# Two mix norms turned by transposes, the attention loop's transposes and masks in another order

## The chip, the cores and the metric

The kernel runs on 1 core of a Trainium2 chip. The time is the device time of one execution in microseconds (us). Engines: TensorE (PE in the rows, its weight loads PEld), VectorE (DVE), ScalarE (ACT), GpSimd (POOL), SyncE (SP), which issues the weight loads from HBM.

## The reference

Three transformer layers over 512 tokens of width 1024, in fp32. The change touches two places of the first two layers. After the mixer of layer 0 (a convolution block) and of layer 1 (attention) comes

```
x = layer_norm(DN_ALPHA * x + mix, ln_mix_g[i], ln_mix_b[i])     # (x - mean) * rsqrt(var + eps) * g + b
ffn = conv_gated_ffn(x, ...)
ple = sigmoid(x @ ple_w_gate[i]) * (p[i] @ ple_w_proj[i])
x = layer_norm(DN_ALPHA * x + ffn + ple, ...)
```

and layer 1 mixes with stick-breaking attention, 16 heads of 64:

```
z = einsum(q, k) * scale;  mask = key < query
log_1m = where(mask, log_sigmoid(-z), 0)
log_a = log_sigmoid(z) + (cumulated log_1m of the later keys)
a = where(mask, exp(log_a), 0);  out = a @ v;  mix = out @ b_wo
```

## The kernel before

**Products.** Each fp32 weight chunk (128x1024) is split into a high and a low part: SP loads `raw`, ScalarE makes `wH` (`high`, L1053), GpSimd `wL` (L416), and TensorE forms three products (L458 to L460, or `by_tokens`, L484 to L486). Four slots hold the chunks, and a chunk's high part is made three chunks ahead: `high_after(c)` waits for the end of chunk c and makes chunk c + 3. Semaphores order everything by hand; each engine runs its list in program order.

**Mix norm** (`mix_norm` on ScalarE, `ple` on TensorE, and a part of VectorE's list; once for layer 0, `mix0`, once for layer 1, `mix1`). The residual stream lies in four blocks of 128 tokens x 1024 (`xr`). For each block VectorE adds the product (L1588), forms the negative mean and writes `xg` = (x - mean) * g (`centre_block`, L1597; the rows call it tmp, whose memory it shares). ScalarE squares the block with its sum (`deviation`, L1129), takes the inverse deviation with Ln and Exp (L1113, L1117), and scales a 128x128 identity by it into `turner` (L1124). TensorE then turns the block to channels x tokens: `turn_block` (L495) does 8 fp32 products of a 128x128 piece of `xg` with `turner`, which divides and turns at once. Blocks 0 and 1 are turned first, then 2 and 3 into the same banks. Out of the banks ScalarE writes the high part `xH` with the shift b added (`high_tiles`, L1170) and VectorE the low part `xL` (`low_tiles`, L1626). Meanwhile TensorE projects p for the four blocks (`project_p`, banks 0 to 3 by turns), and ScalarE keeps each of them in `proj` (`keep`, L1196). Then comes the gate product (`gate`), which needs `xH`, `xL`, all four kept projections and the weight chunks. Off that path VectorE writes the normed stream itself, `xr` = xg * deviation + b (`finish_block`, L1604).

**Attention** (`pair`, once for each of 8 pairs of heads p). On TensorE: `scores` in three parts (`PARTS3`: query tile 3; tiles 2 and 0; tile 1), each part with its masks (a bf16 product into the bank, L723) and its scores (L730), two heads each. Then, for the next pair, the projections of q and k (`project`, 24 products each), `turn_weights(p, 0)` (8 transposes, L742), the projection of v, `turn_weights` 1 and 2 (12 transposes), `turn_values` (4 transposes of v into bank 7, L712), and at last `values`, the weighted sum (L752, L756), which needs all turned weights. On ScalarE: the sigmoids (`chances`, L1325, L1328), copies of q, k, v, of turned weights (`copy_weights`, L1335) and turned v (`copy_values`, L1316), and of the result (`mH`, L1352). On VectorE: the scans (L1755) and the weights (`weigh`, L1762). The last pair has no next pair and fills its waits with small products (`keep_warm`).

Of the kernel before, what the change touches and what calls it, by code (L numbers as in the profile page):

```python
# [8 lines left out]
ACT = mybir.ActivationFunctionType  # L9
ALU = mybir.AluOpType  # L10
# [116 lines left out]
def build_block(nc, ws, xT, xN, pT, params, consts, rope, w1, rows, out):  # L127
    with ExitStack() as ctx:
# [325 lines left out]
        def _(pe):  # L454
# [32 lines left out]

            def turn_block(xname, q, src):

                h = q // 2  # L490
                pe.wait_ge(x_normed, QT * TURN[xname] + q + 1)
                for n in range(KT):
                    bank = ps[TURN_BANKS[xname][h][n // 2]]
                    o = (n % 2) * 2 * P + (q % 2) * P
                    mm = pe.matmul(bank[:, o:o + P], src(q)[:, n * P:n * P + P], turner[:, q, :], start=True, stop=True)  # L495
                    if q % 2 and n % 2:
                        mm.then_inc(x_turned, 1)

            def centred(name):
                def src(q):  # L500
                    pe.wait_ge(x_centred, QT * LN_OF[name] + q + 1)
                    return xg[:, q, :]
                return src

            def updated(q):
                return xr[:, q, :]

            def first_chunks(outs, c, name, xname, src, turn_at, fill):

# [111 lines left out]
            def ple(layer, xname):  # L621

                c0 = CHUNK[f"ple{layer}"]
                full = FULL[("pw2", "wo")[layer]]
                pe.wait_ge(p_ready, layer + 1)
                pe.wait_ge(low_ready, c0 + 2)
                for q in range(2):
                    pe.wait_ge(block_taken, 8 * full + 2 * q + 2)
                    project_p(layer, q).then_inc(proj_done, 1)
                pe.wait_ge(block_taken, 8 * full + 8)  # L630
                src = centred(("pw2", "wo")[layer])
                turn_block(xname, 0, src)
                turn_block(xname, 1, src)
                for q in range(2, QT):
                    pe.wait_ge(proj_kept, QT * layer + q - 1)
                    mm = project_p(layer, q)
                    if q < QT - 1:
                        mm.then_inc(proj_done, 1)
                pe.wait_ge(x_ready, XV[xname] + KT)
                turn_block(xname, 2, src)  # L640
                turn_block(xname, 3, src)

                def gate(k, qs, last=False):
                    c = c0 + 2 + k
                    pe.wait_ge(low_ready, c + 1)
                    for q in qs:
                        t = slice(q * P, q * P + P)
                        for half in range(2):
                            mm = by_tokens(ps[2 * q + half], c % SLOTS, half, xH[:, k, t], xL[:, k, t], k == 0, last)
                            if last and (q, half) != (QT - 1, 1):  # L650
                                mm.then_inc(gate_done, 1)
                    return mm

                pe.wait_ge(proj_kept, QT * layer + QT)
                for k in range(2):
                    pe.wait_ge(x_ready, XV[xname] + k + 1)
                    gate(k, (0, 1))
                pe.wait_ge(x_ready, XV[xname] + 2 * KT)
                for k in range(2):
                    pe.wait_ge(x_ready, XV[xname] + KT + k + 1)  # L660
                    gate(k, (2, 3)).then_inc(chunk_done, 1)
                for k in range(2, KT):
                    pe.wait_ge(x_ready, XV[xname] + KT + k + 1)
                    gate(k, range(QT), k == KT - 1).then_inc(chunk_done, 1)
# [50 lines left out]
            def scores(p, j):  # L715


                for n, tiles in enumerate(PARTS3):
                    if p:
                        pe.wait_ge(bT_ready, 3 * (p - 1) + n + 1)  # L720
                    for h in range(2):
                        for i, (qt, o, w) in enumerate(tiles):
                            pe.matmul(ps[2 * n + h][:, o + w - P:o + w], maskSB, identB, start=i == 0, stop=False,  # L723
                                      skip_group_check=True)
                    if n == 0:
                        pe.wait_ge(qkv_copied, p * 4 + 2)
                    for i, (qt, o, w) in enumerate(tiles):
                        for h in range(2):
                            r = slice(DH * h, DH * h + DH)
                            mm = pe.matmul(ps[2 * n + h][:, o:o + w], qT[r, j, qt * P:qt * P + P], kT[r, j, 0:w],  # L730
                                           start=False, stop=False, skip_group_check=True)
                            if i == len(tiles) - 1:
                                mm.then_inc(z_ready, 1)
# [25 lines left out]
            def pair(p, j, more, first=False):  # L759
                scores(p, j)  # L760
                if more:
                    project(p + 1, 1 - j, 0)
                    project(p + 1, 1 - j, 1)
                    turn_weights(p, 0)
                    project(p + 1, 1 - j, 2)
                    turn_weights(p, 1)
                    turn_weights(p, 2)
                    turn_values(p + 1, 1 - j)
                else:
                    pe.wait_ge(qkv_copied, p * 4 + 4)  # L770
                    keep_warm(7, 30)
                    turn_weights(p, 0)
                    keep_warm(7, 15)
                    turn_weights(p, 1)
                    keep_warm(7, 8)
                    turn_weights(p, 2)
                    keep_warm(7, 6)
                if not first:
                    pe.wait_ge(m_ready, p)
                pe.wait_ge(qkv_copied, p * 4 + 4)  # L780
                values(p, j)

            first_chunks((ps[7], ps[6]), c0, "down0", "ffn0", centred("down0"), (4, 6), 3)
            project(0, 0, 2)
# [261 lines left out]
        def _(act):  # L1046
# [88 lines left out]
            def unit_block(name, q):  # L1135
                deviation(name, q)
                turning_matrix(name, q, 4)

            def post_block(name, q):

                if q < QT - 1:
                    act.wait_ge(block_done, (QT - 1) * FULL[name] + q + 1)
                else:
                    act.wait_ge(chunk_done, CHUNK[name] + dict(COUNTS)[name])
                act.activation(squares[:], banks[:, 2 * q:2 * q + 2, :].rearrange("p a b -> p (a b)"), ACT.Square,  # L1145
                               accum_out=figure(name, q, 3)).then_inc(post_sum, 1)
                act.wait_ge(post_sum, QT * FULL[name] + q + 1)
                inverse_std(name, q, 3, 4, 1)
                act.sem_inc(post_std, 1)
# [36 lines left out]
            def mix_norm(layer):  # L1186
# [13 lines left out]
                    act.wait_ge(res_step, QT)  # L1200
                load_row(f"mix_b{layer}", b_row[:])
                high(c0 + 1)
                for q in range(QT):
                    unit_block(name, q)
                high_after(c0 - 1)
                keep(0)
                high_tiles(xname, 0, 0, 2, shift=f"mix_b{layer}")
                keep(1)
                high(c0 + LEAD)
                high_tiles(xname, 0, 2, 4, shift=f"mix_b{layer}")  # L1210
                keep(2)
                keep(3)
                high_tiles(xname, 1, 0, 4, shift=f"mix_b{layer}")

            def ple(layer):
# [122 lines left out]
            def pair(p, j, more):  # L1338
                for n in range(3):
                    chances(p, n)  # L1340
                if more:
                    copy_qkv(p + 1, 1 - j, 0)
                    copy_qkv(p + 1, 1 - j, 1)
                copy_weights(p, 0)
                if more:
                    copy_qkv(p + 1, 1 - j, 2)
                copy_weights(p, 1)
                copy_weights(p, 2)
                if more:
                    copy_values(p + 1, 1 - j)  # L1350
                act.wait_ge(av_ready, p * 2 + 2)
                act.activation(mH[:, bass.ds(p, 1), :].rearrange("p o t -> p (o t)"), ps[6][:], ACT.Copy)\  # L1352
                    .then_inc(m_high, 1)

            act.sem_inc(q_free, 1)
            for which in range(3):
# [193 lines left out]
        def _(dve):  # L1550
# [43 lines left out]
            def centre_block(name, q):  # L1594
# [2 lines left out]
                dve.scalar_tensor_tensor(xg[:, q, :], xr[:, q, :], figure(name, q, 2), g_row, ALU.add, ALU.mult)\  # L1597
                    .then_inc(x_centred, 1)

            def finish_block(name, q):  # L1600

                dve.wait_ge(post_std, QT * FULL[name] + q + 1)
# [128 lines left out]
                low_tiles("mix0", h, 0, 4, shift="mix_b0")  # L1731
            dve.wait_ge(row_loaded["mix_b0"], 16)
            for q in range(QT):
                finish_block("pw2", q)
            ple(0)
            ffn(0)
            dve.wait_ge(row_loaded["ffn_g0"], 16)
# [50 lines left out]
                low_tiles("mix1", h, 0, 4, shift="mix_b1")  # L1788
            dve.wait_ge(row_loaded["mix_b1"], 16)
            for q in range(QT):  # L1790
                finish_block("wo", q)
            ple(1)
            ffn(1)

# [372 lines left out]
```

## Time and profile before

| | |
|---|---|
| time, median of 3 runs | 2419.19 us (2417.32 to 2421.7) |
| profiled execution | 2417.3 us, its span 2415.5 us |
| busy: PE, DVE, ACT, POOL | 2356.6 (98%), 912.2 (38%), 950.2 (39%), 955.9 (40%) us |
| mean granted clock of TensorE | 0.997 |

Busy time is read from the span between the first and the last instruction; a clock of 1.00 is 2.4 GHz. In a timeline the first number is the start in us from the span's start, the second the length in us of the piece, xN the records merged into it (an fp32 product of TensorE is two records, a transpose one), and in brackets the engine's idle time before it and what ended it.

### The profile page before, as it was taken

The page shows a single profiled execution, that of the slowest core. Times are in us where ns is not written, and L with a number is a line of the kernel's source. Part 1 is how long each engine was busy: PE and PEld are TensorE (multiplying, and loading weights), DVE is VectorE, ACT ScalarE, POOL GpSimd, SP SyncE. Part 2 cuts the span into 40 slices and gives each one's busy share as a digit, 9 for nine tenths or more (in the row PEclk, how much of TensorE's full clock was granted, in tenths as well). Part 3 has the DMA queues.
Part 4 walks back from the last instruction along what each step waited for, and adds up shares of the span by engine and source line. Part 5 has one row for each costly group of instructions (what it writes and reads, how often), then busy time and mean ns, then how long its engine had stood idle before and what let it go on. Part 6 is the DMA issues. An engine that isn't in the chain of part 4 may idle for free.

```text
span 2415.5 us, 30601 instructions
## 1 busy us (share of the span) xinstructions
PE 2356.6 (98%) x11320; PEld 1912.9 (79%) x11320; DVE 912.2 (38%) x1167; ACT 950.2 (39%) x1612; POOL 955.9 (40%) x422
## 2 busy tenths in 40 slices
PE   8989999999999999999999999999999989999998
PEld 6858888888877778888888888888877658888887
DVE  6985344420343323544400422210556862232201
ACT  7764333322454434433322522221534564322222
POOL 5834444444422223444444344444322103444443
PEclk9999999999999999999999999999999999999999
DMA  5212322222212122322222223223312002322222
GB/s 184 70 40 95 119 96 96 96 96 96 88 53 68 64 79 88 113 97 98 99 92 92 89 99 98 96 92 100 146 64 69 28 1 79 105 96 96 96 96 96
DMA packets 58755, 215.17 MB, mean 89 GB/s; under 512 B 6448, under 2 KB 6448, under 8 KB 58416
## 3 DMA queue, kind: packets, MB, share of 16 engines
q1 hardware_dynamic: 55440, 199.83, 24.7%
q10 hardware_dynamic: 3232, 14.16, 1.6%
q8 instruction: 62, 1.02, 0.2%
q14 instruction: 21, 0.17, 0.0%
HBM read 211.86 MB, written 2.10 MB: 89 GB/s over the span
## 4 chain that ended last, share of the span: by engine, by line
PE 87%; DVE 7%; ACT 3%; issue 2%; DMA 1%; SPq 0%; POOL 0%; DVEq 0%; ACTq 0%; POOLq 0%
PE banks L458 17%; PE banks L459 17%; PE banks L460 17%; PE banks L484 9%; PE banks L486 9%; PE banks L485 9%; DVE banks L1708 3%; PE banks L495 1%; PE banks L857 1%; PE banks L730 1%; PE banks L752 1%; PE banks L900 1%; ACT tmp L1473 1%; DMA raw<-ws 1%; PE banks L812 0%
## 5 line engine op out<-in xcount | busy, mean ns | idle before, releaser
L416 POOL TENSOR_TENSOR wL<-raw,wH 128x1024 fp32r<-128x1024 f32 x369 | 892.8, 2421 | 1423.3 <-ACT wH L1053 1423.1
L1053 ACT ACTIVATE wH<-raw 128x1024 fp32r<-128x1024 f32 x371 | 393.2, 1060 | 1108.8 <-PE banks L460 607.1
L458 PE MATMUL banks<-xH,wH 128*128 128x512 f32 (+1 forms) x1976 | 762.7, 386 | 13.3 <-DVE xL L1552 10.8
L459 PE MATMUL banks<-xL,wH 128*128 128x512 f32 (+1 forms) x1976 | 756.2, 383 | 0.0
L460 PE MATMUL banks<-xH,wL 128*128 128x512 f32 (+1 forms) x1976 | 756.1, 383 | 0.0
L458 PEld LDWEIGHTS banks<-xH,wH 128*128 128x128 f32 x1976 | 371.7, 188 | 93.7 <-DVE wL L1557 10.8
L460 PEld LDWEIGHTS banks<-xH,wL 128*128 128x128 f32 x1976 | 371.8, 188 | 72.8
L459 PEld LDWEIGHTS banks<-xL,wH 128*128 128x128 f32 x1976 | 371.9, 188 | 71.5 <-issue 0.7
L484 PE MATMUL banks<-wH,hH 128*128 128x512 f32 x704 | 274.2, 389 | 3.5 <-DVE tmp L1666 3.5
L486 PE MATMUL banks<-wL,hH 128*128 128x512 f32 x704 | 273.9, 389 | 0.0
L485 PE MATMUL banks<-wH,hL 128*128 128x512 f32 x704 | 273.9, 389 | 0.0
L1668 DVE TENSOR_TENSOR hL<-tmp,hH 128x512 f32 x88 | 206.0, 2341 | 98.3 <-ACT hH L1257 98.3
L1666 DVE TENSOR_TENSOR tmp<-banks,tmp 128x512 f32<-128x512 f32 x88 | 60.9, 692 | 365.2 <-PE banks L460 354.0
L484 PEld LDWEIGHTS banks<-wH,hH 128*128 128x128 f32 x704 | 132.1, 188 | 32.4 <-issue 5.1
L485 PEld LDWEIGHTS banks<-wH,hL 128*128 128x128 f32 x704 | 132.2, 188 | 27.4
L486 PEld LDWEIGHTS banks<-wL,hH 128*128 128x128 f32 x704 | 132.2, 188 | 27.3
L1659 DVE SCALAR_TENSOR_TENSOR tmp<-banks,par,tmp 128x511 f32<-128x511 f32 x88 | 65.9, 749 | 139.2 <-ACT tmp L1247 132.5
L1588 DVE SCALAR_TENSOR_TENSOR xr<-xr,banks 128x512 f32<-128x512 f32 x32 | 20.6, 680 | 259.1 <-PE banks L486 259.1
L1612 DVE TENSOR_TENSOR banks<-banks,tmp 128x512 f32<-128x512 f32 x24 | 15.5, 692 | 259.5 <-ACT squares L1145 259.2
L1708 DVE SCALAR_TENSOR_TENSOR banks<-gpad,par,banks 128x512 f32<-128x512 f32 x112 | 75.1, 750 | 1.1 <-DVE tmp L1682 0.9
L484 PE MATMUL banks<-wH,xH 128*128 128x512 f32 x192 | 75.0, 390 | 0.0
L486 PE MATMUL banks<-wL,xH 128*128 128x512 f32 x192 | 74.7, 389 | 0.0
(247 smaller groups left out, 2275.1 us busy)
## 6 DMA issues: line engine op xcount, KB each, us to landing
raw<-ws SPq DMA_DIRECT2D x371, 512.0 KB, 3.6
w1b<-w ACTq DMA_DIRECT2D x2, 2048.0 KB, 11.4
tmp<-rows ACTq DMA_DIRECT2D x7, 512.0 KB, 3.3
b_row<-rows ACTq DMA_DIRECT2D x5, 512.0 KB, 4.4
tmp<-xT SPq DMA_DIRECT2D x8, 256.0 KB, 7.4
xr<-xN ACTq DMA_DIRECT2D x1, 2048.0 KB, 8.6
out<-xr SPq DMA_DIRECT2D x4, 512.0 KB, 2.6
pf<-pT ACTq DMA_DIRECT2D x2, 512.0 KB, 3.8
```

The source lines that it names most:

```text
L416: pool.tensor_tensor(wL[:, j, :], raw[:, j, :], fp(wH[:, j, :]), ALU.subtract).then_inc(low_ready, 1)
L458: pe.matmul(bank, wH[:, slot, cols], rh, start=start, stop=False)
L459: pe.matmul(bank, wH[:, slot, cols], rl, start=False, stop=False)
L460: return pe.matmul(bank, wL[:, slot, cols], rh, start=False, stop=stop)
L484: pe.matmul(bank, rh, wH[:, slot, w], start=start, stop=False)
L485: pe.matmul(bank, rl, wH[:, slot, w], start=False, stop=False)
L486: return pe.matmul(bank, rh, wL[:, slot, w], start=False, stop=stop)
L1053: act.activation(wH[:, c % SLOTS, :], raw[:, c % SLOTS, :], ACT.Copy).then_inc(high_ready, 1)
L1659: dve.scalar_tensor_tensor(tmp[:, j, back:S], ps[4 + 2 * j][:, 0:S - back], pc(f"fcw{inst}", f * FCONV_W + tap), tmp[:, j, back:S], ALU.mu ...
L1666: dve.tensor_tensor(tmp[:, 2 + j, :], ps[5 + 2 * j][:], tmp[:, j, :], ALU.mult).then_inc(h_made, 1)
L1668: dve.tensor_tensor(hL[:, bass.ds(f, 1), :].rearrange("p o t -> p (o t)"), tmp[:, 2 + j, :], fp(hH[:, bass.ds(f, 1), :].rearrange("p o t - ...
L1708: ins = dve.scalar_tensor_tensor(dst, g, w, sums[i % 2], ALU.mult, ALU.add)
```

## The change

In the mix norms ScalarE multiplies the centred block by the deviation (`divide_block`), TensorE turns it with a plain transpose against the identity, and VectorE adds b to it for the stream (`shift_block`). ScalarE's list in `mix_norm` is ordered anew. In the attention the three `turn_weights` follow each other ahead of the third projection, `turn_values` and its copy come behind `values` and the copy of the result, and the masks of all three parts stand together ahead of the scores.

```diff
@@ turn_block
+                    if src is divided:
+                        mm = pe.transpose(bank[:, o:o + P], xg[:, q, n * P:n * P + P], cc("ident"))
+                    else:
+                        mm = pe.matmul(bank[:, o:o + P], src(q)[:, n * P:n * P + P], turner[:, q, :], start=True, stop=True)
...
@@ ple, TensorE
-                src = centred(("pw2", "wo")[layer])
-                turn_block(xname, 0, src)
-                turn_block(xname, 1, src)
+                turn_block(xname, 0, divided)
+                turn_block(xname, 1, divided)
...
-                turn_block(xname, 2, src)
-                turn_block(xname, 3, src)
+                turn_block(xname, 2, divided)
+                turn_block(xname, 3, divided)
@@ scores
+                if p:
+                    pe.wait_ge(bT_ready, 3 * p)
                 for n, tiles in enumerate(PARTS3):
-                    if p:
-                        pe.wait_ge(bT_ready, 3 * (p - 1) + n + 1)
                     for h in range(2):
                         for i, (qt, o, w) in enumerate(tiles):
                             pe.matmul(ps[2 * n + h][:, o + w - P:o + w], maskSB, identB, start=i == 0, stop=False,
                                       skip_group_check=True)
-                    if n == 0:
-                        pe.wait_ge(qkv_copied, p * 4 + 2)
+                pe.wait_ge(qkv_copied, p * 4 + 2)
+                for n, tiles in enumerate(PARTS3):
                     for i, (qt, o, w) in enumerate(tiles):
@@ pair, TensorE
-                    turn_weights(p, 0)
+                    for n in range(3):
+                        turn_weights(p, n)
                     project(p + 1, 1 - j, 2)
-                    turn_weights(p, 1)
-                    turn_weights(p, 2)
-                    turn_values(p + 1, 1 - j)
...
                 values(p, j)
+                if more:
+                    turn_values(p + 1, 1 - j)
@@ ScalarE
+            def divide_block(name, q):
+
+                deviation(name, q)
+                act.wait_ge(x_centred, QT * LN_OF[name] + q + 1)
+                act.activation(xg[:, q, :], xg[:, q, :], ACT.Copy, scale=figure(name, q, 4)).then_inc(x_normed, 1)
@@ mix_norm
-                for q in range(QT):
-                    unit_block(name, q)
+                for q in range(3):
+                    divide_block(name, q)
+                keep(0)
+                divide_block(name, 3)
+                keep(1)
                 high_after(c0 - 1)
-                keep(0)
-                high_tiles(xname, 0, 0, 2, shift=f"mix_b{layer}")
-                keep(1)
-                high(c0 + LEAD)
-                high_tiles(xname, 0, 2, 4, shift=f"mix_b{layer}")
+                high_tiles(xname, 0, 0, 4, shift=f"mix_b{layer}")
                 keep(2)
                 keep(3)
+                high(c0 + LEAD)
                 high_tiles(xname, 1, 0, 4, shift=f"mix_b{layer}")
@@ pair, ScalarE
-                copy_weights(p, 0)
+                for n in range(3):
+                    copy_weights(p, n)
                 if more:
                     copy_qkv(p + 1, 1 - j, 2)
-                copy_weights(p, 1)
-                copy_weights(p, 2)
-                if more:
-                    copy_values(p + 1, 1 - j)
                 act.wait_ge(av_ready, p * 2 + 2)
                 act.activation(mH[:, bass.ds(p, 1), :].rearrange("p o t -> p (o t)"), ps[6][:], ACT.Copy)\
                     .then_inc(m_high, 1)
+                if more:
+                    copy_values(p + 1, 1 - j)
@@ VectorE
+            def shift_block(xname, q):
+
+                dve.wait_ge(x_normed, QT * TURN[xname] + q + 1)
+                dve.tensor_tensor(xr[:, q, :], xg[:, q, :], b_row[:], ALU.add).then_inc(res_step, 1)
...
-                finish_block("pw2", q)
+                shift_block("mix0", q)
...
-                finish_block("wo", q)
+                shift_block("mix1", q)
```

## Rows read from the trace of the kernel before

**Rows 1.** The page, chain that ended last, by engine.
```profile
PE 87%; DVE 7%; ACT 3%; issue 2%; DMA 1%; SPq 0%; POOL 0%; DVEq 0%; ACTq 0%; POOLq 0%
```
**Rows 2.** Timeline of TensorE in one pair of the attention; start, length.
```profile
712.38 2.16 PE L752 MATMUL banks<-bT,vN 128*64 128x384 f32 x16 [1.38 <-ACT bT L1335]
...
714.69 0.28 PE L723 MATMUL banks<-bcon 128*128 128x128 bf16 x2
714.90 1.13 PE L730 MATMUL banks<-kT,qT 64*128 64x512 f32 x4
715.96 0.40 PE L723 MATMUL banks<-bcon 128*128 128x128 bf16 x4
716.29 1.14 PE L730 MATMUL banks<-kT,qT 64*128 64x384 f32 x8
717.36 0.28 PE L723 MATMUL banks<-bcon 128*128 128x128 bf16 x2
...
718.21 0.50 PE L458 MATMUL banks<-xH,wH 128*128 128x512 f32 x1
...
729.24 1.04 PE L742 MATMUL banks<-con,beta 128*128 128x128 f32 x8
...
735.70 1.47 PE L742 MATMUL banks<-con,beta 128*128 128x128 f32 x12
737.00 0.60 PE L712 MATMUL banks<-con,vT 128*128 128x128 f32 x4
738.98 0.54 PE L752 MATMUL banks<-bT,vN 128*64 128x384 f32 x2 [1.38 <-ACT bT L1335]
```
**Rows 3.** Waits of TensorE from 650 to 905 us: in total, times, longest.
```profile
PE banks L752 <- ACT bT L1335: 9.7, 7, 1.4
```
**Rows 4.** Timeline of VectorE and ScalarE in the same pair.
```profile
725.80 0.73 DVE L1762 TENSOR_TENSOR beta<-banks,beta 128x255 f32<-128x255 f32 x2
...
738.72 0.61 ACT L1316 ACTIVATE vN<-banks 128x512 f32<-128x512 f32 x1
```
**Rows 5.** Timeline of TensorE in the first mix norm.
```profile
218.74 3.73 PE L495 MATMUL banks<-turner,tmp 128*128 128x128 f32 x32
...
227.76 3.73 PE L495 MATMUL banks<-turner,tmp 128*128 128x128 f32 x32
...
231.25 0.48 PE L484 MATMUL banks<-wH,xH 128*128 128x512 f32 x1
```
**Rows 6.** Timelines of ScalarE, VectorE and GpSimd in the first mix norm.
```profile
208.30 1.13 ACT L1129 ACTIVATE squares<-xr,stat 128x1024 f32<-128x1024 f32 x1
209.34 0.18 ACT L1129 ACTIVATION_READ_ACCUMULATOR squares<-xr,stat 128x1 f32 x1
...
210.22 0.41 ACT L1124 ACTIVATE turner<-con,stat 128x128 f32<-128x128 f32 x1
210.53 1.14 ACT L1129 ACTIVATE squares<-xr,stat 128x1024 f32<-128x1024 f32 x1
...
219.43 1.00 ACT L1196 ACTIVATE proj<-banks 128x1024 f32<-128x1024 f32 x1
...
230.19 3.03 ACT L1170 ACTIVATE xH<-banks,par 128x256 fp32r<-128x256 f32 x8 [1.21 <-PE banks L495]
...
231.07 3.23 DVE L1626 SCALAR_TENSOR_TENSOR xL<-banks,par,xH 128x256 fp32r<-128x256 f32 x8 [4.04 <-ACT xH L1170]
...
224.68 2.40 POOL L416 TENSOR_TENSOR wL<-raw,wH 128x1024 fp32r<-128x1024 f32 x1 [2.72 <-ACT wH L1053]
```
**Rows 7.** Timelines of ScalarE and TensorE in the second mix norm.
```profile
904.14 1.13 ACT L1129 ACTIVATE squares<-xr,stat 128x1024 f32<-128x1024 f32 x1
...
923.55 3.73 PE L495 MATMUL banks<-turner,tmp 128*128 128x128 f32 x32
```
**Rows 8.** Groups by form: busy us, mean ns of one, idle before and its cause.
```profile
L1643 DVE TENSOR_TENSOR tmp<-tmp,proj 128x1024 f32<-128x1024 f32 x8 | 18.6, 2320 | 63.9 <-issue 63.9
```
**Rows 9.** Windows: length, then busy us (records) of each engine, clock, DMA share, GB/s.
```profile
735.00:739.00 4.00, 2.62 (x22) 2.23 (x20) 0.00 (x0) 3.11 (x5) 1.49 (x1) 1.00 0.38 131
```

More of the change, by code:

```diff
@@ L494, in turn_block @@
                     o = (n % 2) * 2 * P + (q % 2) * P
-                    mm = pe.matmul(bank[:, o:o + P], src(q)[:, n * P:n * P + P], turner[:, q, :], start=True, stop=True)
+                    if src is divided:
+                        mm = pe.transpose(bank[:, o:o + P], xg[:, q, n * P:n * P + P], cc("ident"))
+                    else:
+                        mm = pe.matmul(bank[:, o:o + P], src(q)[:, n * P:n * P + P], turner[:, q, :], start=True, stop=True)
                     if q % 2 and n % 2:
@@ L506, in updated, with divided @@
                 return xr[:, q, :]
+            def divided(q):
+                return xg[:, q, :]
             def first_chunks(outs, c, name, xname, src, turn_at, fill):
```

## The prediction, made before the change was run

> **What bounds the kernel now.** I read the page first, then the waits of TensorE, then the two stretches that the change touches as a timeline. The chain that ended last is TensorE's for 87% of the span [rows 1], so an edit is worth what it takes out of TensorE's own order of work: instructions there, or waits there. Work of ScalarE, VectorE and GpSimd counts only where TensorE waits for it.
>
> In the attention loop one pair takes 738.98 - 712.38 = 26.6 us, seven pairs of eight alike. TensorE's row shows four bits of mask and score work, then 729.24 - 718.21 = 11.0 us of two projections, 8 turned weight tiles, the third projection, 12 turned tiles, 4 turned values, and then a hole before the weighted values start at 738.98 [rows 2]. The hole is the only wait of that loop that TensorE has on another engine: 1.4 us, seven times, for the copy of the turned weights, 9.7 us in all [rows 3]. The copy can't come sooner, because its transposes are the last thing before the values.
>
> At the mix norm TensorE never waits. It turns two token blocks from 218.74, projects for two blocks, turns the other two from 227.76, and starts the gate at 231.25 [rows 5]. Those turnings are ordinary fp32 products against a scaled identity: 16 of them (32 records, two passes each) in 231.25 - 227.76 = 3.49 us, 0.218 us each.
>
> **Part 1, values behind the third projection.** The transposes of parts 1 and 2 move ahead of the projection, so their copies on ScalarE lie under it: three, of at most 1.00 us each by the copy of 128x1024 from PSUM in [rows 6], against half of the 11.0 us of two projections, 5.5. The values then start with no wait. The turned v moves behind the values. From the start of the v transposes to the start of the values is now 738.98 - 737.00 = 1.98 us; of this the four transposes themselves are 4 x 0.108 = 0.43 us (12 transposes take 737.00 - 735.70 = 1.30 us) [rows 2]. What is left is 1.55; I take 1.5, since the transition to the next kind of product must be paid once. 7 pairs x 1.5 = **10.5 us**. Bounds: the wait alone, 9.7, and 7 x 1.55 = 10.9.
>
> What is late next? The transposes of parts 1 and 2 now need VectorE's weights earlier, straight after part 0's. VectorE ends its last weights at 725.80 + 0.73 = 726.53, TensorE arrives at 729.24 [rows 2, 4]: 2.7 us in hand. The masks put together push the first finished scores back by about 0.35 us and bring TensorE's arrival forward by 0.6, so 1.7 us remain, and parts 0 and 1 have more. Behind the values, ScalarE copies mH and then the turned v, two copies of 128x512 at 0.61 us each (the v copy's row in [rows 4]), before the next pair's sigmoids. It is through some 1.3 us after the values end. Until the first scores of the next pair TensorE needs 0.43 us of transposes, 0.57 of masks (below) and half or all of 1.06 of scores, 1.5 to 2.1 us, so the sigmoids wait for scores and not for the copies. The projection that reuses bank 7 comes over 3 us after the values. The high parts of weights behind each projection keep their places and run three chunks ahead; SP's loads follow the same counter.
>
> **Part 2, masks together.** Starts in [rows 2]: a group of two masks takes 714.90 - 714.69 = 0.21 us, one of four 716.29 - 715.96 = 0.33. So a mask costs 0.06 and a group 0.09. The scores: two heads of 512 columns 1.06, two of 384 and two of 128 (as many columns, twice the instructions) 1.07, two of 256 columns 718.21 - 717.36 - 0.21 = 0.64 [rows 2]. The second and the first differ by nothing, the third gives 0.42 us for 256 columns, and so 0.22 us belong to the group, not to its columns or instructions. Three groups of each become one: 2 x (0.09 + 0.22) = 0.62 us less a pair. Eight pairs, the last too: **4.9 us**. Below, if the cost of a group is a fill of the array that the scores of each part pay anyhow: 0; no row shows grouped masks. I take the upper value, because the scores of part 1 already show two tiles behind each other without a second such cost.
>
> **Part 3, the mix norms (twice).** A turning by transpose costs what one of the attention costs, 0.108 us; 16 of them 1.73 against 3.49 us. Four such stretches would give 4 x 1.76 = 7.0 us if TensorE could use it all. The records of the second site carry the same length, 3.73 us for 32 [rows 5, 7].
>
> ScalarE pays. It now multiplies a 128x1024 block by the deviation where it scaled a 128x128 identity. Before, the scaling costs 210.53 - 210.22 = 0.31 us of its order, the nearest row of the new shape is the square of the same block: its next instruction starts 209.34 - 208.30 = 1.04 later [rows 6]. So a block, now 210.53 - 208.30 = 2.23 us, takes 2.96. From 208.30: three blocks to 217.18, first projection kept (about 1.0, the row at 219.43) to 218.15, block 3's square and figures 1.92 to 220.07, its scaling to 221.11, second projection kept to 222.1, the weights' high part to 223.05, and eight tiles in 3.03 to 226.1. VectorE's last low tile ends 1.08 us behind ScalarE's last (234.30 against 233.22) [rows 6], so 227.16. TensorE: first turning ends at 218.74 + 1.73 = 220.5, two projections take 5.53 (227.76 less 218.74 + 3.49), the second turning could start at 226.0 but gets its banks at 227.2 to 227.4. A wait of about 1.3 us is new. The gate starts at 229.15 in place of 231.25: 2.1 us. In the second norm the first square lies 923.55 - 904.14 = 19.4 us before the second turning [rows 7], here 227.76 - 208.30 = 19.5, so the same gain. **4.2 us** together. Bounds: 7.0 with no wait, 2.5 if each step of ScalarE is 0.1 us longer than taken.
>
> Two edits cost nothing. The chunk whose high part is made behind the third and fourth kept projections, later than now, is ready on ScalarE at about 229.1 and on GpSimd 2.4 us later (row at 224.68) at 231.6 [rows 6]; the gate asks for it at 229.15 + 2.76 = 231.9. That is 0.3 us, the thinnest cover of the change: without it each us of lateness is a us of the time, twice. VectorE's last pass, a sum of two SBUF tiles in place of a multiply and add, may take 2.3 us as the product of the same shape does, but VectorE stands idle 32 us behind it [rows 8]; four of them fit.
>
> **The sum** is 10.5 + 4.9 + 4.2 = 19.6 us. The profiled execution took 2417.3 us, its span 2415.5 and 1.8 around it; so 2397.7. The median of the runs is 2419.19, 1.9 above it: forecast **2399.6 us**.
>
> **A rule that speaks against it.** In [rows 9] the stretch with 16 transposes and the hole behind them, over 3 us without one ordinary product, has a granted clock of 1.00, the level of 2.4 GHz, and what follows runs at the same pace. The Trainium skill (TensorE: Matmul & The Clock Gate, Part 4: PE-mode transpose) says that a transpose doesn't count as work of TensorE for the clock in the way a matmul does. By that rule 20 in a row, or 16 where products stood, could drop it; by the row they don't, since the longest such stretch of the new order (20 transposes, 2.2 us) is shorter than the one shown.
>
> **Rivals.** A, masks together give nothing: 19.6 - 4.9, so 2404.5. For it: the price of a group is read from three differences; against: two pairs of them agree.
> B, the norms give nothing, because ScalarE and the thin cover on GpSimd eat the shorter turnings: 2403.8. For it, the 0.3 us; against, that ScalarE would have to come 2 us later than its rows add up to.
> C, the wait moves to the transposes of parts 1 and 2, because VectorE's weights come late: if all of the hole comes back, 2417.3 - 9.1, so about 2410 in the median. It needs VectorE 1.7 + 1.5 us later than its rows.
> D, slower: the clock falls to 1.2 GHz in the runs of transposes. Twice 64 x 0.108 (norms) and twice 7 x 20 x 0.108 (weights) add 22 us, more than the 19.6 won, and each ordinary product behind them that runs slow comes on top; 2.5 us of these and the kernel is slower than 2424. Against it is the row of part 1's hole.
>
> **How the numbers follow.** Forecast 0.64, A 0.14, B 0.09, C 0.04, D 0.04, and 0.05 for what I haven't seen, split over small gain and none. About 0.2%, 4.8 us, is what a measurement of this kernel can tell from no change. The forecast, A, B and C are all beyond it on the fast side: 0.91; within 0.05; slower 0.04. The range: at its fast end all upper bounds, 10.9 + 4.9 + 7.0 = 22.8, give 2419.2 - 22.8 = 2396.4; at its slow end A with the lower norms, 10.5 + 0 + 2.5, gives 2406.2. About 1.5 us for the spread of the runs goes on both ends. 2395 to 2408.
>
> **What would show it.** Right: no idle of TensorE before the weighted values in seven pairs; a pair in 26.6 - 2.1 = 24.5 us; eight masks in 0.57 us and the scores in 2.3; turnings of 16 records in about 1.8 us; an idle of about 1.3 us before the second turning, put down to VectorE's low tiles. Wrong: TensorE waiting for beta before a transpose, waiting for GpSimd in the gate, scores as long as now, or a clock below 1.00 in a window of the loop. The prediction fails if a wait that I place on ScalarE's side lands on TensorE in every pair.

## The result, and the profile after

The changed kernel takes 2398.69 us (median of 4 runs, 2397.98 to 2399.91), the kernel before 2418.26 in the same series (4 runs, 2416.87 to 2421.7). The ratio is 0.9918, 95% interval 0.9900 to 0.9935: 19.6 us less. The profiled execution took 2399.91 us, its span 2398.1.

The page, the chain that ended last (beside [rows 1]):

```profile
PE 92%; ACT 4%; DVE 3%; DMA 1%; issue 1%; SPq 0%; DVEq 0%; ACTq 0%
```

**One pair of the attention.** The timeline of TensorE, as in [rows 2]:

```profile
708.91 0.66 PE L718 MATMUL banks<-con,vT 128*128 128x128 f32 x4
709.41 0.61 PE L729 MATMUL banks<-bcon 128*128 128x128 bf16 x8
709.95 2.43 PE L736 MATMUL banks<-kT,qT 64*128 64x512 f32 x16
712.30 0.50 PE L458 MATMUL banks<-xH,wH 128*128 128x512 f32 x1
...
723.33 2.35 PE L748 MATMUL banks<-con,beta 128*128 128x128 f32 x20
725.43 0.48 PE L458 MATMUL banks<-xH,wH 128*128 128x512 f32 x1
...
731.08 2.16 PE L758 MATMUL banks<-bT,vN 128*64 128x384 f32 x16
733.39 0.66 PE L718 MATMUL banks<-con,vT 128*128 128x128 f32 x4
```

From one turning of v to the next it is 733.39 - 708.91 = 24.48 us, where it was 26.6. No bracket stands behind the values: the hole is gone. Eight masks begin at 709.41 and the scores at 709.95, so 0.54 us for the masks; the scores take 712.30 - 709.95 = 2.35. Together 2.89 where six pieces took 3.52 [rows 2]. The list of waits from 650 to 905 us, where [rows 3] had seven of 1.4 us, now holds one wait in all, at the first turning of v, which the kernel before has too:

```profile
PE banks L718 <- ACT vT L1321: 0.7, 1, 0.7
```

VectorE and ScalarE in the same pair (beside [rows 4]):

```profile
720.85 0.73 DVE L1778 TENSOR_TENSOR beta<-banks,beta 128x255 f32<-128x255 f32 x2
...
709.06 0.60 ACT L1361 ACTIVATE mH<-banks 128x512 fp32r<-128x512 f32 x1 [0.81 <-PE banks L762]
709.61 0.60 ACT L1328 ACTIVATE vN<-banks 128x512 f32<-128x512 f32 x1
711.11 1.09 ACT L1337 ACTIVATE beta<-banks 128x512 f32<-128x512 f32 x2 [0.90 <-PE banks L736]
```

VectorE ends its weights at 721.58 and TensorE asks for them at 723.33: 1.75 us in hand. The sigmoids wait 0.90 us for TensorE's scores, not for the two copies ahead of them.

**The mix norms.** TensorE in the first and in the second (as [rows 5] and [rows 7]):

```profile
219.83 1.91 PE L497 MATMUL banks<-con,tmp 128*128 128x128 f32 x16
221.50 0.48 PE L484 MATMUL banks<-wH,pH 128*128 128x512 f32 x1
...
228.58 1.97 PE L497 MATMUL banks<-con,tmp 128*128 128x128 f32 x16 [1.39 <-DVE xL L1642]
230.30 0.48 PE L484 MATMUL banks<-wH,xH 128*128 128x512 f32 x1
...
897.96 1.91 PE L497 MATMUL banks<-con,tmp 128*128 128x128 f32 x16
906.29 1.97 PE L497 MATMUL banks<-con,tmp 128*128 128x128 f32 x16 [0.94 <-DVE xL L1642]
908.01 0.48 PE L484 MATMUL banks<-wH,xH 128*128 128x512 f32 x1
```

A turning takes 221.50 - 219.83 = 1.67 us where it took 3.49. From the first turning to the gate it is 230.30 - 219.83 = 10.47 us, before 231.25 - 218.74 = 12.51 [rows 5]: 2.04 less. In the second norm it is 908.01 - 897.96 = 10.05 us, before 12.52: 2.47 less. The bracket at 228.58 is a new wait, for VectorE's low tiles.

ScalarE, VectorE and GpSimd there (as [rows 6]):

```profile
209.53 1.14 ACT L1135 ACTIVATE squares<-xr,stat 128x1024 f32<-128x1024 f32 x1
...
211.44 1.15 ACT L1149 ACTIVATE tmp<-tmp,stat 128x1024 f32<-128x1024 f32 x1
212.50 1.13 ACT L1135 ACTIVATE squares<-xr,stat 128x1024 f32<-128x1024 f32 x1
...
234.13 4.62 DVE L1614 TENSOR_TENSOR xr<-tmp,b_row 128x1024 f32<-128x1024 f32 x4
...
230.30 2.41 POOL L416 TENSOR_TENSOR wL<-raw,wH 128x1024 fp32r<-128x1024 f32 x1 [3.28 <-ACT wH L1059]
234.17 6.83 POOL L416 TENSOR_TENSOR wL<-raw,wH 128x1024 fp32r<-128x1024 f32 x1 [1.46 <-ACT wH L1059]
```

The multiplication costs ScalarE 212.50 - 211.44 = 1.06 us of its order, a block 212.50 - 209.53 = 2.97. GpSimd's split of the gate's second chunk ends at 232.71, 0.3 us before the gate asks for it (230.30 + 2.76 = 233.06). The next split, of the gate's third chunk, takes 6.83 us instead of 2.4: it began 0.04 us behind the first of four sums of VectorE (4.62 us in one piece), and 4.58 + 2.25 is its length. In the kernel before, VectorE's four multiply-adds stand in the place of the sums, from 234.21, and the same split, begun just as close behind the first of them, takes 3.49 us:

```profile
234.25 3.49 POOL L416 TENSOR_TENSOR wL<-raw,wH 128x1024 fp32r<-128x1024 f32 x1 [7.17 <-ACT wH L1053]
```

That I had not expected, and the experiments return to it.

**A yardstick without the clock.** From the first turning of the first mix norm to the first turning at the end of layer 1, both kernels run at a granted clock of 1.00, so this distance D tells more than one whole execution. Its end in the kernel before, then in the changed one:

```profile
1331.96 2.02 PE L495 MATMUL banks<-turner,xr 128*128 128x128 f32 x16 [0.57 <-ACT turner L1124]
```
```profile
1312.95 2.02 PE L499 MATMUL banks<-turner,xr 128*128 128x128 f32 x16 [0.57 <-ACT turner L1130]
```

D was 1331.96 - 218.74 = 1113.22 us and is 1312.95 - 219.83 = 1093.12: **20.1 us less**. Two more profiled executions of the changed kernel gave 1093.07 and 1093.09. The two spans differ by only 17.4, for two reasons outside D. The start took 1.1 us longer (the first turning at 219.83 and not 218.74): the clock rose later in it, and from 143.1 us on some eight products stood 0.43 us apart, which in the kernel before they don't. That is no doing of the change, whose three profiled executions reach this turning at 217.96, 219.83 and 220.89. And late in the kernel, in layer 2, the windows (length, busy time of each engine, granted clock) read, before and then after:

```profile
1900.00:1920.00 20.00, 18.24 (x170) 13.84 (x168) 18.81 (x38) 13.80 (x40) 0.00 (x0) 0.91 0.01 2
```
```profile
1883.00:1903.00 20.00, 18.35 (x156) 12.93 (x152) 17.79 (x37) 14.47 (x39) 0.00 (x0) 0.83 0.00 1
```

The same work had 0.91 in one execution and 0.83 in the other; the rest of the kernel behind the attention took 1.6 us longer. Over the runs of the kernel before the mean clock is 0.993 to 0.998 and the time tends to go with it: 2423.11 to 2424.96 us in the three at 0.993 and 0.994, 2415.91 to 2420.36 from 0.996 on. So a median of four or five runs is uncertain by 1 to 2 us. D repeats much better: within 0.05 us in three executions of the changed kernel, within 0.14 in two of a version below. The kernel before and each part alone were profiled once, so their D stands on one execution each.

### The profile page after: what moved, and what is told of

Its sections match the earlier page's. It is cut to its first block, busy times and chain, and to the rows that moved or that the text cites. A ratio compares the mean times of both kernels' runs of the same rounds, so it can differ in the third digit from the quotient of the medians.

```text
span 2398.1 us, 30463 instructions
## 1 busy us (share of the span) xinstructions
PE 2347.0 (98%) x11256; PEld 1905.8 (79%) x11256; DVE 907.7 (38%) x1167; ACT 955.5 (40%) x1612; POOL 962.4 (40%) x422
## 4 chain that ended last, share of the span: by engine, by line
PE 92%; ACT 4%; DVE 3%; DMA 1%; issue 1%; SPq 0%; DVEq 0%; ACTq 0%
PE banks L458 18%; PE banks L459 18%; PE banks L460 18%; PE banks L484 9%; PE banks L486 9%; PE banks L485 9%; PE banks L863 1%; DMA raw<-ws 1%; PE banks L499 1%; PE banks L906 1%; PE banks L736 1%; PE banks L748 1%; PE banks L758 1%; PE banks L687 1%; PE banks L688 1%; PE banks L689 1%
```

## Experiments

"Changed" is the changed kernel, a line with + or - is an edit to it. Each comparison has the kernel before in the same series: 2418.94 us for the first four (21 runs), 2418.86 for the next four (9), 2418.84 for the two after (14), 2418.20 for the last two (9).

### Each part alone

The masks together, with the rest as before:

```diff
@@ turn_block, ple, mix_norm, VectorE's list, pair, copies: as in the kernel before
@@ scores: as changed
                 if p:
                     pe.wait_ge(bT_ready, 3 * p)
                 for n, tiles in enumerate(PARTS3):
                     for h in range(2):
                         ...
                 pe.wait_ge(qkv_copied, p * 4 + 2)
```

> The kernel before with only the masks put together. By the price of a group (0.22 us for scores, 0.09 us for masks, two groups fewer of each) each of the eight pairs is 0.62 us shorter: 4.9 us in all, about 2413.4 by the median of 2418.3, and in the trace masks and scores of a pair take 2.9 us in place of 3.52. If the group's price is a fill of the array that each part pays anyhow (rival A), the time stays at 2418.3 and the stretch at 3.5 us.

Measured: 2413.96 us (11 runs, 2411.47 to 2415.96), ratio 0.9979, 0.9970 to 0.9988: 5.0 less. D is 1108.89: 4.3 less. TensorE:

```profile
711.96 2.16 PE L752 MATMUL banks<-bT,vN 128*64 128x384 f32 x16 [1.38 <-ACT bT L1335]
...
714.27 0.62 PE L723 MATMUL banks<-bcon 128*128 128x128 bf16 x8
714.82 2.43 PE L730 MATMUL banks<-kT,qT 64*128 64x512 f32 x16
...
738.06 2.16 PE L752 MATMUL banks<-bT,vN 128*64 128x384 f32 x16 [1.38 <-ACT bT L1335]
```

Masks and scores are short as in the changed kernel and the hole is all there. The pair takes 738.06 - 711.96 = 26.10 us, 0.50 less and not 0.62. The rest is in the projections: the third takes 5.63 us where it took 5.56 [rows 2], the first two together 11.06 for 11.03. The third takes 5.63 to 5.65 in every edited kernel looked at, the changed one too (731.08 - 725.43), and I have no cause for it.

The new order of the pair alone:

```diff
@@ turn_block, ple, mix_norm, VectorE's list, scores: as in the kernel before
@@ pair, TensorE: as changed
                     for n in range(3):
                         turn_weights(p, n)
                     project(p + 1, 1 - j, 2)
@@ behind values: as changed, the copies on ScalarE in the same order
                 if more:
                     turn_values(p + 1, 1 - j)
```

> The kernel before with only the transposes, the projection, the values and their copies in the new order. By my theory the hole before the values goes, 1.5 us in each of seven pairs: 10.5 us less, about 2407.8, and TensorE waits for nothing in the loop. Rival C: TensorE waits for VectorE's weights before the transposes of parts 1 and 2, and part or all of the 9.7 us comes back (2410 to 2418).

Measured: 2407.04 us (4 runs, 2405.57 to 2408.95), ratio 0.9956, 0.9941 to 0.9971: 11.9 less. D is 1102.59: 10.6 less, 7 x 1.52. TensorE's waits from 650 to 905 us hold no line for the values:

```profile
PE banks L712 <- ACT vT L1309: 0.7, 1, 0.7
```

The norms alone:

```diff
@@ scores, pair, copies in the attention: as in the kernel before
@@ turn_block, ple, mix_norm, divide_block, shift_block: as changed
```

> The changed kernel with the attention put back as it was before, so only the norms are changed. Theory: 4.2 us less by the prediction's sum, 4.5 by the changed kernel's trace (12.51 less 10.47 and 12.52 less 10.05 us from the first turning to the gate), so about 2413.9. Rival B: the norms give nothing, 2418.3.

Measured: 2413.97 us (10 runs, 2409.79 to 2416.91), ratio 0.9976, 0.9967 to 0.9986: 5.0 less. D is 1109.24: 4.0 less. The stretches themselves give 2.2 and 2.4; some 0.5 is lost in the attention, whose order this kernel leaves as it was: a pair takes 26.68 us there and not 26.60, the third projection again 5.64. The second turnings wait as in the changed kernel:

```profile
227.69 1.97 PE L497 MATMUL banks<-con,tmp 128*128 128x128 f32 x16 [1.27 <-DVE xL L1643]
```

The three parts add up to 18.9 us of D; together they give 20.1. So none takes from another. Most of the 1.2 us between is the longer third projection, some 0.08 us a pair: each part alone pays it, together they pay it once (2 x 7 x 0.08 = 1.1). And each of the rivals that gave a part nothing (A and B) is out by both measures.

### Is it the transpose or the new order of the norm?

The turnings as ordinary products against the identity; ScalarE's and VectorE's lists stay as changed.

```diff
@@ turn_block
-                        mm = pe.transpose(bank[:, o:o + P], xg[:, q, n * P:n * P + P], cc("ident"))
+                        mm = pe.matmul(bank[:, o:o + P], xg[:, q, n * P:n * P + P], cc("ident"), start=True, stop=True)
```

> The changed kernel with the blocks of the mix norms turned by an ordinary fp32 product against the identity in place of the transpose; all else as changed. If the transposes carry the gain of the norms: a turning of 16 pieces takes 3.49 us again in place of 1.67, the wait before the second turning closes (0 to 0.1 us), and each norm loses what it won, 2.0 and 2.5 us: about 2403.2 against 2398.7 of the changed kernel. If ScalarE's new order carries it: 2398.7.

Measured: 2404.59 us (4 runs, 2402.77 to 2405.45), ratio 0.9942, 0.9927 to 0.9958. D is 1097.58, 4.5 above the changed kernel. TensorE in the first norm:

```profile
218.46 3.73 PE L497 MATMUL banks<-con,tmp 128*128 128x128 f32 x32
227.49 3.73 PE L497 MATMUL banks<-con,tmp 128*128 128x128 f32 x32
```

32 records again, and no wait ahead of the second turning: from the start of the first it is 9.03 us, before 9.02 [rows 5]. So the norms' gain is the transposes' and nothing else's, and the division on ScalarE is hidden as long as TensorE is slow. 4 x 1.82 = 7.3 us of shorter turnings, less waits of 1.39 and 0.94, gives 5.0; 4.5 was there. In the first norm the difference is the wait's measure: a bracket counts from the modelled end of a product, from start to start the wait is 1.54, and the turning behind it takes 1.72 us and not 1.67.

### The new wait, and GpSimd's long split

Three kernels and the changed one again. In the first the four sums of VectorE wait until GpSimd has split the gate's third chunk, so that they can't hold it up there. In the second VectorE, idle at that time, does the first two copies of the projections (`keep`) in place of ScalarE. The third is both.

```diff
@@ shift_block, VectorE (first and third)
+                dve.wait_ge(low_ready, CHUNK[f"ple{xname[-1]}"] + 5)
                 dve.wait_ge(x_normed, QT * TURN[xname] + q + 1)
@@ mix_norm, ScalarE (second and third)
-                keep(0)
                 divide_block(name, 3)
-                keep(1)
@@ VectorE, ahead of low_tiles (second and third)
+            def keep(layer, q):
+                dve.wait_ge(proj_done, (QT - 1) * layer + q + 1)
+                dve.tensor_copy(proj[:, q, :], banks[:, 2 * (q % 2):2 * (q % 2) + 2, :].rearrange("p a b -> p (a b)"))\
+                    .then_inc(early_kept, 1)
```

> The changed kernel once more, on the chip and among the runs of the three that follow, so that they can be compared with it: 2398.7, 19.6 us below the kernel before.

> The changed kernel with VectorE's sum of two SBUF tiles (four of 128x1024 behind each mix norm) held until GpSimd has made the low part of the gate's third chunk. In the changed kernel that GpSimd instruction takes 6.8 us in place of 2.4 and ends at 241.0, 0.2 us before the gate asks for it at 241.2. If the four sums lock it out: it takes 2.4 us here. The time stays at 2398.7, since the cover still held.

> The same without holding the sums. TensorE reaches the gate's third chunk 1.5 us sooner, while GpSimd is locked out of it until about 240 by the four sums: TensorE then waits 0.2 to 1 us there in each norm, and the time is 0.4 to 2 us above that of the run with the sums held, 2396.9 to 2398.5. If the lock costs nothing: both alike, 2396.5.

> The changed kernel with the first two kept projections copied by VectorE, idle for 6.5 us there, in place of ScalarE, and its sums held as in the run with the sums later. ScalarE's tiles come 1.8 us sooner, the wait of TensorE before the second turning (1.39 and 0.94 us) goes, less 0.1 us of waiting in the gate for the second chunk: 2.0 to 2.4 us less than the changed kernel, 2396.5. If ScalarE's list is not what makes the wait: 2398.7.

Measured:

| kernel | median, runs | ratio, interval | D |
|---|---|---|---|
| changed again | 2397.95, 5 (2396.24 to 2399.47) | 0.9911, 0.9898 to 0.9925 | 1093.07 |
| sums later | 2398.13, 5 (2396.28 to 2401.11) | 0.9918, 0.9904 to 0.9931 | 1092.86 |
| copies on VectorE | 2394.65, 4 (2393.27 to 2397.55) | 0.9905, 0.9890 to 0.9920 | 1091.42 |
| both | 2397.73, 4 (2395.68 to 2398.82) | 0.9911, 0.9896 to 0.9926 | 1091.20 |

GpSimd, then VectorE, with the sums later:

```profile
232.23 2.39 POOL L416 TENSOR_TENSOR wL<-raw,wH 128x1024 fp32r<-128x1024 f32 x1 [1.46 <-ACT wH L1059]
...
237.97 2.50 POOL L416 TENSOR_TENSOR wL<-raw,wH 128x1024 fp32r<-128x1024 f32 x1 [3.34 <-ACT wH L1059]
...
234.72 6.84 DVE L1615 TENSOR_TENSOR xr<-tmp,b_row 128x1024 f32<-128x1024 f32 x4 [2.44 <-issue]
```

The split is back at 2.39 us, so it was the sums that stretched it to 6.83. Now GpSimd's next split begins at 237.97, 0.24 us before the third sum ends, and takes only 2.50: it gets in, and the fourth sum takes 3.42 us in place of 1.22, the four 6.84 in place of 4.62. The Trainium skill (SBUF — State Buffer, section "Who interferes with whom") says that a VectorE instruction with two SBUF inputs contends with a GpSimd instruction that reads SBUF, and that whichever issues first blocks the other for its length; the fourth sum here, 2.2 us longer by one split of 2.4, agrees. Who comes next when several instructions follow each other is not in it, and the rows give no single answer. A split begun 0.04 us behind the first sum had to let all four pass, in both norms of every profiled kernel that has the sums without the hold; one begun in the third sum got in ahead of the fourth; and in the kernel before one begun behind the first multiply-add got in ahead of the second (3.49 us). What decides between these I don't know. For the time it is worth 0.2 us of D, little more than D's own spread: the changed kernel's cover was only just enough.

With the copies on VectorE the wait before the second turning is gone. The two stretches from first turning to gate take 8.87 and 8.90 us instead of 10.47 and 10.05, 2.75 less, yet D falls by 1.6 only. The rest comes back inside the gate. Weight loads of TensorE there:

```profile
229.43 0.19 PEld L487 LDWEIGHTS banks<-wL,xH 128*128 128x128 f32 x1
230.16 0.19 PEld L485 LDWEIGHTS banks<-wH,xH 128*128 128x128 f32 x1 [0.54 <-DVE xL L1647]
...
238.00 0.19 PEld L487 LDWEIGHTS banks<-wL,xH 128*128 128x128 f32 x1
238.47 0.19 PEld L485 LDWEIGHTS banks<-wH,xH 128*128 128x128 f32 x1 [0.28 <-issue]
```

Where the pitch is 0.23, one load comes 0.73 behind the last and one 0.47; the first 80 steps of the gate take 18.80 us and not 18.30, so 0.5 us per norm. The first hole stands 12 products into the gate, where its second chunk is asked for. The bracket names VectorE, but GpSimd's split of that chunk ends at 227.64 + 2.40 = 230.04 us, and in the two other profiled executions with this edit the same place in the second norm has GpSimd in the bracket, in that of "both":

```profile
908.50 0.47 PE L485 MATMUL banks<-wH,xH 128*128 128x512 f32 x1 [0.15 <-POOL wL L417]
```

The second stands 48 products in, at the third chunk, whose split falls into the four sums; with the sums held it is gone. So the gate, 1.6 us earlier, has used up both covers on GpSimd: the wait moved and went away only in part. "Both" was expected 2.0 to 2.4 us below the changed kernel and is 1.9 below it in D, and the copies alone 0.4 to 2 us above "both": 0.2 in D, while the medians of four stand the other way about, 3.1 us apart. To see whether the time itself tells the two kernels apart, both were run once more side by side.

> The same kernel as in the run before under this name: the two early copies of the projections on VectorE. Theory: the norm stretches are 10.47 + 10.05 - 8.87 - 8.90 = 2.75 us shorter than in the changed kernel, so 2.7 us less in the median, some 2395.5 to 2396. Rival: the third chunk's late split gives back 0.3 us per norm beyond what the stretches show and the spread of the clock made up the rest of the first difference; then 2 us or less, about 2396.8.

> The changed kernel as it is, beside the version with the early copies on VectorE, for a comparison in the same series: 2398 to 2399 by the two medians so far (2398.69 and 2397.95).

Measured: 2395.68 us (4 runs, 2394.83 to 2397.86), ratio 0.9907, 0.9892 to 0.9922, D 1091.56; changed 2396.46 (5 runs, 2395.57 to 2399.01), ratio 0.9915, 0.9902 to 0.9929, D 1093.09. All runs of both series together: 2395.7 (8 runs) against 2397.3 (10). The version with the copies on VectorE is ahead by 1.6 us in D and in these medians, but the intervals overlap by far; 0.07% is seen in the traces and not proved by the times. My 2.7 us was too much, the rival's "2 or less" right.

### How thin is GpSimd's cover?

The prediction put the cover of the gate's second chunk at 0.3 us. Here ScalarE makes its high part behind the last eight tiles, some 3 us later.

```diff
@@ mix_norm, ScalarE
-                high(c0 + LEAD)
                 high_tiles(xname, 1, 0, 4, shift=f"mix_b{layer}")
+                high(c0 + LEAD)
```

> The changed kernel with the high part of the gate's second weight chunk made behind ScalarE's last eight tiles, about 3 us later. The prediction called the cover of this chunk 0.3 us and said that beyond it each us of lateness is a us of the time, twice. By this: GpSimd has the low part 2.9 us later, TensorE waits some 2.7 us in the gate of each norm, about 5.4 us more than the changed kernel: 2404.1. If there is other cover: 2398.7 and no wait in the gate.

Measured: 2418.73 us, ratio 0.9994, 0.9984 to 1.0004 (9 runs from 2416.32 to 2419.72; a tenth run of 5575.76 us, for which I have no cause, is left out of that range): 20 us above the changed kernel, the whole gain, where 5.4 was expected. D is 1112.34, 19.2 more. GpSimd, VectorE and TensorE:

```profile
233.57 9.11 POOL L416 TENSOR_TENSOR wL<-raw,wH 128x1024 fp32r<-128x1024 f32 x2 [6.96 <-ACT wH L1059]
...
233.54 4.62 DVE L1614 TENSOR_TENSOR xr<-tmp,b_row 128x1024 f32<-128x1024 f32 x4
...
240.51 0.77 PE L484 MATMUL banks<-wH,xH 128*128 128x512 f32 x1 [7.59 <-POOL wL L416]
241.07 0.63 PE L485 MATMUL banks<-wH,xL 128*128 128x512 f32 x1
241.50 0.63 PE L486 MATMUL banks<-wL,xH 128*128 128x512 f32 x1
...
245.25 0.40 PE L486 MATMUL banks<-wL,xH 128*128 128x512 f32 x1
245.48 0.39 PE L484 MATMUL banks<-wH,xH 128*128 128x512 f32 x1
```

Three things add up. The split starts late, at 233.57; alone it would end 2.4 us later, and TensorE, which asks at 232.76, would wait 3.2. But the four sums began 0.03 us ahead of it, so it ends 2.35 us behind them (233.54 + 4.62 + 2.35 = 240.51, the moment TensorE goes on): 4.5 us more. And after the hole of 7.59 us the products come 0.43 us apart, not 0.23, up to 244.9. That is the level of 1.2 GHz (the window from 240 to 260 us has a granted clock of 0.87), ten products, 2 us. From the first turning to the gate's 80th step this norm takes 9.8 us more than in the changed kernel; the second has a wait of 7.6 us too and only some seven products at the lower level, 9.3 us more. Together that is the 19.2 us of D.

### Can a run of transposes lower the clock?

Forty unused transposes are put ahead of each third projection, right behind the twenty of the weights.

```diff
@@ project
+                if p and which == 2:
+                    for _ in range(40):
+                        pe.transpose(ps[7][:, 0:P], cc("ident"), cc("ident"))
```

> The changed kernel with 40 more transposes of the identity in each of seven pairs, ahead of the third projection and right behind the 20 of the weights; their result is not used. Theory: a transpose costs 0.108 us and the granted clock stays at 2.4 GHz: 7 x 40 x 0.108 = 30.4 us more than the changed kernel, 2429.1, products behind them at 0.227 us each. Rival D: in a run of 60 transposes (6.5 us) the clock falls to 1.2 GHz; then transposes and the products behind them take twice as long, over 2440, and the windows of the loop show a granted clock below 1.00.

Measured: 2427.61 us (5 runs, 2426.39 to 2429.94), ratio 1.0037, 1.0023 to 1.0052: 29 us above the changed kernel. TensorE, and a window over it (1.00 is the granted clock):

```profile
701.93 2.35 PE L751 MATMUL banks<-con,beta 128*128 128x128 f32 x20
704.12 4.53 PE L715 MATMUL banks<-con 128*128 128x128 f32 x40
708.40 0.48 PE L458 MATMUL banks<-xH,wH 128*128 128x512 f32 x1
708.72 0.39 PE L459 MATMUL banks<-xL,wH 128*128 128x512 f32 x1
```
```profile
690.00:715.00 25.00, 25.00 (x149) 20.89 (x148) 8.87 (x14) 11.10 (x21) 4.77 (x2) 1.00 0.13 43
```

Sixty transposes stand in 6.5 us without one ordinary product, and the clock stays at 1.00; the next products take their usual 0.39. The forty cost 708.40 - 704.12 = 4.28 us, 0.107 each, as transposes at full clock; 7 x 4.28 = 30.0; D is 1123.69, 30.6 more. In late_chunk 7.6 us without work did lower it. The Trainium skill (TensorE: Matmul & The Clock Gate, Part 4: PE-mode transpose) says that a transpose doesn't count as work of TensorE in the same way; the rows here don't bear that out for a clock that is already at its upper level. Whether transposes alone would raise it no run here shows.

## Why the prediction was right

It said 2399.6 us, 19.6 below the median shown then; measured were 2398.69, and 19.6 below the kernel before in the same series. The mechanism of each part held; that the differences agree to a tenth is luck, since the ratio's interval spans 16 to 24 us and D says 20.1. By terms:

| step | predicted | in the traces |
|---|---|---|
| values behind the third projection | 7 x 1.5 = 10.5 | 7 x 1.50 = 10.5 from the pairs, 10.6 in D alone |
| masks together | 8 x 0.62 = 4.9 | 0.63 for masks and scores of a pair; alone 0.50 a pair, 4.3 in D |
| mix norms | 2 x 2.1 = 4.2 | 2.04 + 2.47 = 4.5; alone 4.0 in D |
| new wait at the second turning | 1.3 | 1.39, 0.94 (first norm in two more executions 1.19, 1.24) |
| VectorE's weights in hand | 1.7 | 1.75 |
| cover of the gate's second chunk | 0.3 | 0.3 |

**The values.** Right as put: the hole of 1.4 us and 0.1 of a switch go, the copies lie under the projection, and nothing comes late in their place. Rival C falls, with 1.75 us in hand.

**The masks.** The price of a switch, read out of differences between groups that no row showed alone, held: 0.54 for eight masks (0.57 predicted), 2.35 for the scores (2.3). Rival A falls.

**The norms.** The block's 2.96 us on ScalarE was 2.97. The second norm gained 0.4 more than "the same gain": its wait was 0.94. A small surprise within this step: the third division waited 0.41 us, behind its own figures by the bracket, in the first norm of each of its executions and not in the second. Rival B falls, since the stretches are 2.04 and 2.47 us shorter.

**The clock.** Rival D falls by direct test, with three times the run of transposes that the change has.

**What it had wrong, without harm.** Two sentences on GpSimd's cover. That VectorE's last pass costs nothing was argued from VectorE's idle time alone. Its four sums are quick, 4.62 us where up to 2.3 each were allowed, but they shut GpSimd out for 4.6 us: the split of the gate's third chunk takes 6.83 us, 3.49 in the kernel before, and it is through at 241.0, when the gate, 48 products in, asks at about 230.30 + 4 x 2.73 = 241.2: 0.2 us of cover, thinner than the one I named as thinnest. And "each us of lateness is a us of the time, twice" is undersized: a chunk late by 3 us cost 9.6 a norm, by the sums ahead of it and by the clock behind it. So the chance of 0.09 for rival B, whose price was the norms' 4.2 us, hid a case in which the whole change comes back. It was near: late_chunk differs by one instruction's place. The prediction also reads six pieces of masks and scores as four; nothing in its sum rests on that.

## What to carry to other kernels

When a consumer waits for a copy of what was turned just ahead of it, put the next long independent product between them, and the turning of the next step behind the consumer; one look at who has time in hand (here 1.75 us) tells if the wait only moves. A transpose instead of an fp32 product with a scaled identity halves the turning, but once TensorE is faster, the engine that feeds it sets the pace: of 7.3 us, 4.5 came through. Where GpSimd's work has a cover of tenths, look at which two-input instructions of VectorE stand together next to it, and judge small differences by a distance within the trace at full clock, not by four medians.

## What the runs showed of the hardware

- Four VectorE sums of two SBUF tiles in a row stretch a GpSimd split begun 0.04 us behind the first from 2.4 to 6.83 us; behind the first of four multiply-adds it takes 3.49. Begun in the third sum, the split takes 2.50 and stretches the fourth from 1.22 to 3.42.
- TensorE's transposes of 128x128 fp32 run 0.104 to 0.108 us apart, in one record, against 0.218 us for an fp32 product of the same size in two; 60 in a row leave the clock at 1.00.
- A hole of 7.59 us was followed by 4.4 us of products 0.43 us apart, the holes of 1.39 us and less in the attention and before the second turnings by none. Between them it is no matter of length alone: among the convolution's products a hole of 1.96 us in the changed kernel's execution (to 142.35) was followed by some, one of 2.46 us in the execution before (to 141.99) by none.
- Eight bf16 masks in one group and all scores behind them take 2.89 us, in three groups 3.52: a switch to and fro costs about 0.31 us.
- The mean clock of one and the same kernel differs from run to run, 0.993 to 0.998, and its time by up to 9 us, while a distance of 1093 us at 1.00 repeats within 0.05 us in three executions, one of 1091 within 0.14 in two.
